# Re-ordering the opening, the scan's first steps and the output projection of a three-block model, with eight idle matmuls at the start

## The chip, the cores and the metric

The kernel runs on one core of one Trainium2 chip. The metric is the device time of one execution in microseconds. A core has five engines with queues of their own: TensorE (PE; its weight loads are shown as PEld), VectorE (DVE), ScalarE (ACT), GpSimd (POOL) and SyncE (SP), which issues the weight transfers. They wait for each other through semaphores that the kernel sets and waits for by hand.

## What is computed

Two token-mixing blocks with their MLPs, and then a third block, over 256 tokens (272 with 16 meta tokens in front) of width 1024, all in float32. What the change touches lies in the first mixer, a state-space one, and in the attention of the second, which works on query blocks of 16, 128 and 128 tokens; h is rms-normed ahead of both:

```python
def ssd_mixer(h, w_in, conv_w, conv_b, dt_bias, a_log, d_skip, norm_g, w_out):
    zxbcdt = h @ w_in
    z, xbc, dt = jnp.split(zxbcdt, [SSD_D_INNER, SSD_D_INNER + SSD_CONV_DIM], axis=-1)
    xbc = jax.nn.silu(causal_depthwise_conv(xbc, conv_w, conv_b))
    dt = jax.nn.softplus(dt.astype(f32) + dt_bias.astype(f32))
    ...
    decay = jnp.exp(jnp.where(causal, a_cs[..., :, None] - a_cs[..., None, :], -jnp.inf))
    cb = jnp.einsum('bclgn,bcsgn->bcgls', c_c, b_c)
    y_diag = jnp.einsum('bcgjls,bcsgjp->bclgjp', cb[:, :, :, None] * decay, xdt)
    ...
    g = (y * jax.nn.silu(z)).reshape(bsz, L, SSD_GROUPS, SSD_D_INNER // SSD_GROUPS)
    g = g * lax.rsqrt(jnp.mean(g * g, axis=-1, keepdims=True) + EPS)
    return (g.reshape(bsz, L, SSD_D_INNER) * norm_g) @ w_out

def mla_mixer(h, ...):
    ...
    p = jax.nn.softmax(jnp.where(mask, sc, -jnp.inf), axis=-1)
    outs.append(jnp.einsum('bhqk,bkhd->bqhd', p, v[:, :e]))
```

## The kernel before

Activations lie with features on the 128 partitions and tokens along the row. Every large product is made three times, in a reduced float32 format: a value is split into a high part (rounded by ACT) and a low part (what is left, a subtraction on DVE or POOL), and `tile` (L446) issues high x high, high x low and low x high (L458 to L460) for each of the 8 steps of the inner dimension. One *page* is 128 output columns of weights: 512 KB, loaded by SP into one of four slots of `w_raw`, split by `hi` (ACT, L942) and `lo` (DVE L1379, POOL L1998), and read by 24 matmuls. There are 344 pages, in one fixed order. The slot's next load waits for `lo`, its next `hi` for the matmuls (`w_used`). `lin_chunk` takes two pages into one half of the PSUM tile `lin`; the other half is drained meanwhile (`drained`, by the chunk's parity).

**The opening.** h arrives in four transfers. ACT rounds each of its 8 tiles (`xr_hi`, in the memory of `g_hi`, L974) and squares it (L955), DVE makes the low parts (`raw_lo`, L1411) and adds the squares up in fours (`add_squares`, L1415). PE makes the dt columns (24 matmuls of 32 rows, L500 to L502), with two matmuls by ones for the norm's sum between them (`first_stat`, L490), and two pages of x, all from the un-normed h. Then `norm_inv` (ACT L965, L967) gives `r_inv`, and DVE and ACT make the normed input `x_hi`, `x_lo` (L1402, L984, L1406) that all later chunks read.

**The scan** has 8 groups in slots 0 to 7, three chunks each (x; B and C; z), and runs one group's later steps beside the next group's projections; `slot` on each engine writes that order out by hand. The steps that matter here are: `conv0` (ACT L1019) and `conv` (DVE L1481) drain a chunk; `clamp` (L1491), `sigmoid` (ACT L1000 to L1004) and `silu` (L1495) follow; `cb_products` and `x_transposes` (PE); `decay_logs` (ACT L1033) reads `acs_bc`, which POOL fetches by a transfer for each group (`acs_rows`, L2006) once the group before has used it; `decay` (L1043), `head_mix` (L1519) and `y_products` (PE L558 to L564), whose third step has 16 tokens only; and a norm per group (`group_stat` L545, `g_low` L1525). A slot begins on PE with a chunk that waits until `conv` of the slot before has drained its half of `lin`.

**The output projection** (`sout`) reads groups 0 to 3 as half 0 and 4 to 7 as half 1, and stops 2 steps short of the end of half 1 until the last group's norm is done. DVE then adds the result to h (`add_pair`, L1601).

**Values of the attention** (`values`, L778 to L782) have a first step over 16 key tokens.

## Time and profile before

| | us |
|---|---|
| median of 3 runs (1121.63 to 1124.04) | 1123.45 |
| the profiled execution | 1122.35 |
| its span, first to last instruction | 1120.7 |
| PE busy in the span | 1095.9 |
| DVE, ACT, POOL busy | 769.1, 655.1, 165.3 |

The profiled execution lies 1.1 us under the median, and 1.65 us of it lie outside the span. PE is busy in nearly all of the span, so time is lost where PE stands still or runs at its lower clock. Of the 40 equal slices of the span (28 us each), only the first (6 tenths), the second (8) and the last (8) show PE below nine tenths. The mean granted clock over the span is 0.997, and the stretches from 30 to 40 us and from 40 to 50 us have 0.83.

A row of the timeline reads: start in us, length in us, engine, line, operation, output<-input, shape, and in brackets how long the engine had stood still before and what ended that. Matmuls are pipelined, so the step from one start to the next, not the length, is what one costs.

### The profile page before, as it was taken

Reading aid. Unit: us, or ns where it says so; the run is one execution under the profiler, and the core shown is the slowest. Engines: PE = TensorE matmul, PEld = TensorE weight load, DVE = VectorE, ACT = ScalarE, POOL = GpSimd, SP = SyncE. Lnnn points to the kernel's source line nnn. Section 1 sums busy time; section 2 is a strip of 40 time slices with the busy share of each in tenths; the row PEclk is TensorE's granted clock in tenths of the full one; section 3 lists DMA queues with packets and bytes.
Section 4 is the critical chain, followed back from the end, with each engine's and each line's share of the span. In section 5 each row is a group of like instructions: output and inputs, shape, how many; then the busy total and the mean of one; then the engine's idle time right before and its main releaser. Section 6 shows DMA issues by size and latency. Waiting matters only on the chain.

```text
span 1120.7 us, 23950 instructions
## 1 busy us (share of the span) xinstructions
PE 1095.9 (98%) x8935; PEld 1064.0 (95%) x8935; DVE 769.1 (69%) x1156; ACT 655.1 (58%) x1077; POOL 165.3 (15%) x150
## 2 busy tenths in 40 slices
PE   6899999999999999999999999999999999999998
PEld 6899999899999999988799999999989999999998
DVE  7789989868665455588686665557787587666543
ACT  7699998655545444477565554446546656555332
POOL 0344444408000000112020000000003201000000
PEclk9899999999999999999999999999999999999999
DMA  6444454484545554433255555555444555555552
GB/s 229 161 164 170 152 189 151 129 252 165 185 170 170 178 178 167 153 132 113 77 188 188 183 183 183 188 182 176 171 135 156 175 185 188 184 180 188 184 185 92
DMA packets 53226, 189.96 MB, mean 170 GB/s; under 512 B 5920, under 2 KB 7200, under 8 KB 53168
## 3 DMA queue, kind: packets, MB, share of 16 engines
...
q8 instruction: 38, 0.62, 0.2%
...
## 4 chain that ended last, share of the span: by engine, by line
PE 73%; DVE 11%; ACT 9%; issue 4%; DMA 1%; POOL 1%; ACTq 1%; DVEq 0%; SPq 0%; POOLq 0%
PE lin L458 22%; PE lin L460 22%; PE lin L459 22%; DVE w_lo L1379 3%; ACT w_hi L942 2%; DVE cv L1481 1%; ACT dd L1033 1%; DVE sg L1491 1%; DMA acs_bc<-acs_dram 1%; ACT cv L1019 1%; PE lin L676 1%; ACT sg L1002 1%; PE lin L677 1%; PE lin L678 1%; ACT ee L1043 1%
## 5 line engine op out<-in xcount | busy, mean ns | idle before, releaser
L1379 DVE TENSOR_TENSOR w_lo<-w_raw,w_hi 128x1024 fp32r<-128x1024 f32 (+3 forms) x318 | 383.9, 1209 | 254.1 <-ACT w_hi L942 254.0
L942 ACT ACTIVATE w_hi<-w_raw 128x1024 fp32r<-128x1024 f32 (+2 forms) x342 | 352.1, 1034 | 224.8 <-PE lin L460 222.1
L458 PE MATMUL lin<-x_hi,w_hi 128*128 128x256 f32 (+1 forms) x1504 | 433.7, 288 | 6.0 <-DVE cv L1481 2.7
L460 PE MATMUL lin<-x_hi,w_lo 128*128 128x256 f32 (+1 forms) x1504 | 429.7, 286 | 0.0
L459 PE MATMUL lin<-x_lo,w_hi 128*128 128x256 f32 (+1 forms) x1504 | 428.8, 285 | 0.0
L458 PEld LDWEIGHTS lin<-x_hi,w_hi 128*128 128x128 f32 x1504 | 285.0, 189 | 8.3 <-POOL w_lo L1998 2.9
L460 PEld LDWEIGHTS lin<-x_hi,w_lo 128*128 128x128 f32 x1504 | 285.2, 190 | 0.0
L459 PEld LDWEIGHTS lin<-x_lo,w_hi 128*128 128x128 f32 x1504 | 284.5, 189 | 0.6
L460 PE MATMUL lin<-hid_hi,w_lo 128*128 128x256 f32 (+1 forms) x768 | 218.2, 284 | 0.0
L459 PE MATMUL lin<-hid_lo,w_hi 128*128 128x256 f32 (+1 forms) x768 | 217.9, 284 | 0.0
L458 PE MATMUL lin<-hid_hi,w_hi 128*128 128x256 f32 (+1 forms) x768 | 217.4, 283 | 0.0
L460 PEld LDWEIGHTS lin<-hid_hi,w_lo 128*128 128x128 f32 x768 | 145.1, 189 | 0.0
L458 PEld LDWEIGHTS lin<-hid_hi,w_hi 128*128 128x128 f32 x768 | 145.0, 189 | 0.0
L459 PEld LDWEIGHTS lin<-hid_lo,w_hi 128*128 128x128 f32 x768 | 144.3, 188 | 0.0
L1990 POOL TENSOR_TENSOR h_sq<-h_sq 128x256 f32<-128x256 f32 (+1 forms) x35 | 30.7, 876 | 451.8 <-ACT h_sq L955 450.4
L1122 ACT ACTIVATE relu<-lin 128x512 f32<-128x512 f32 (+1 forms) x48 | 29.1, 606 | 82.6 <-PE lin L460 82.6
L1998 POOL TENSOR_TENSOR w_lo<-w_raw,w_hi 128x1024 fp32r<-128x1024 f32 x24 | 60.0, 2499 | 86.5 <-ACT w_hi L942 86.3
L951 ACT ACTIVATE x_hi<-h,vecs 128x256 fp32r<-128x256 f32 (+2 forms) x40 | 20.3, 507 | 43.2 <-DVE h L1642 38.3
L458 PE MATMUL lin<-g_hi,w_hi 128*128 128x272 f32 x144 | 42.5, 295 | 2.1 <-DVE g_lo L1525 1.0
L1625 DVE TENSOR_TENSOR hid_lo<-relu_sq,hid_hi 128x512 f32 (+1 forms) x48 | 34.4, 717 | 11.2 <-DVE relu_sq L1621 11.2
L460 PE MATMUL lin<-g_hi,w_lo 128*128 128x272 f32 x144 | 41.7, 289 | 0.0
L459 PE MATMUL lin<-g_lo,w_hi 128*128 128x272 f32 x144 | 41.5, 288 | 0.0
...
## 6 DMA issues: line engine op xcount, KB each, us to landing
w_raw<-w SPq DMA_DIRECT2D x342, 512.0 KB, 3.3
...
```

The costliest lines, as they stand in the source:

```text
L458: mm3(o, wh, xh, start=first and i == 0, stop=False)
L459: mm3(o, wh, xl, start=False, stop=False)
L460: ins = mm3(o, wl, xh, start=False, stop=last and i == kts - 1)
L676: mm3(o, lh, wh, start=i == 0, stop=False)
L677: mm3(o, ll, wh, start=False, stop=False)
L942: a(w_hi[pg.slot][:, 0:n], w_raw[pg.slot][:, 0:n], ACT.Copy).then_inc(w_hi_done, pages)
L951: a(x_hi[:, kt.value, 0:width(norm)], h[:, kt.value, tokens(norm)], ACT.Copy, scale=gain(norm, kt.value)).then_inc(xh_done, 1)
L1122: a(relu[i][:, :, 0:n], linp(k, slice(0, n)), ACT.Relu).then_inc(drained[k.parity], 1)
L1379: tt(w_lo[pg.slot][:, 0:n], w_raw[pg.slot][:, 0:n], w_hi[pg.slot][:, 0:n].bitcast(F32), ALU.subtract)\
L1625: tt(hid_lo[:, bass.ds(at.value, 2), 0:n], relu_sq[i][:, :, 0:n], hid_hi[:, bass.ds(at.value, 2), 0:n].bitcast(F32), ALU.subtract).then_in ...
L1990: tt(h_sq[:, 0, 0:n], h_sq[:, 0, 0:n], h_sq[:, kt, 0:n], ALU.add).then_inc(hsum_done, 1)
L1998: tt(w_lo[pg.slot][:, 0:n], w_raw[pg.slot][:, 0:n], w_hi[pg.slot][:, 0:n].bitcast(F32), ALU.subtract)\
```

## The change

It has four parts.

**Opening.** PE first issues eight matmuls of ones by ones into `ps4`, whose result nobody reads, and then sums the norm itself: eight matmuls, one for each tile of squares, ahead of the dt columns; two of the squares are made by DVE, six by ACT, and the additions on DVE are gone. ACT makes most of the rounded tiles before the squares, and `norm_inv` comes ahead of the split of page 3. The dt steps on DVE move in between the low parts of the normed input. x of group 0 is scaled into two PSUM banks, not into `y2`. DVE, not POOL, makes the low part of page 7 (second page of z of group 0); POOL instead makes that of page 8, and fetches `acs_bc` first.

**First slots.** Slot 0 has an order of its own (`first_slot`): on DVE both convolutions come one after the other, then the clamps; on ACT the pages' splits come first, then the sigmoids. The `decay_logs` of group 0 move from the end of slot 0 into slot 1.

**Output projection.** `group_stat(At(7))` comes one tile earlier, the fourth tile stops after 3 steps of half 1 and makes its other 5 at the end, and DVE's first `add_pair` comes ahead of a page's low part.

**16-row steps.** `x_tok[:, 2, :]` and `p_t0` are zero below their 16 rows, and the last step of `y_products` and the first of `values` read all 128 rows.

```diff
+WARM = 8
-        first_xs = y2
+        first_xs = (ps5, ps6)
-        p_t0 = [sb(f"p_t0{i}", [META, T2], F32, mla) for i in range(2)]
+        p_t0 = [sb(f"p_t0{i}", [P, T2], F32, mla) for i in range(2)]
...
             pe.wait_ge(ones_set, 1)
+            for i in range(WARM):
+                nc.tensor.matmul(ps4[:, 0:P], ones0, ones0, start=True, stop=True)
+            for kt, (squared, count) in enumerate(((hsq_done, 1), (hsq_done, 2), (hsq_dve, 1), (hsq_dve, 2),
+                                                   (hsq_done, 3), (hsq_done, 4), (hsq_done, 5), (hsq_done, 8))):
+                pe.wait_ge(squared, count)
+                ins = nc.tensor.matmul(ps7[:, 0:T], ones0, h_sq[:, kt, :], start=kt == 0, stop=kt == KD - 1)
+            ins.then_inc(stat_done, 1)
             pe.wait_ge(w_lo_done[0], 1)
-                if kt in (2, 3):
-                    first_stat(kt - 2)
...
-                        ins = nc.tensor.matmul(o[rows, 256:T], x_tok[0:META, 2, j * HD:(j + 1) * HD],
-                                               mm[0:META, j, 416:432], start=False, stop=True)
+                        ins = nc.tensor.matmul(o[rows, 256:T], x_tok[:, 2, j * HD:(j + 1) * HD],
+                                               mm[:, j, 416:432], start=False, stop=True)
...
             pe.wait_ge(gl_done, 14)
-            for j in range(3):
-                sout(0, j, 1, 0, 6)
-            group_stat(At(7))
-            sout(0, 3, 1, 0, 6)
+            sout(0, 0, 1, 0, 6)
+            sout(0, 1, 1, 0, 6)
+            group_stat(At(7))
+            sout(0, 2, 1, 0, 6)
+            sout(0, 3, 1, 0, 3)
             pe.wait_ge(gl_done, 16)
-            for j in range(4):
+            for j in range(3):
                 sout(0, j, 1, 6, 2)
+            sout(0, 3, 1, 3, 5)
...
                 if has_lin and early:
-                    if s.base:
-                        hi((c + 2).page(0))
+                    hi((c + 2).page(0))
                     conv0(s, 0)
+                    decay_logs(g, 0)
+                    hi((c + 2).page(1))
+                    decay_logs(g, 1)
...
+            def first_slot():
+                s, c = At(0), At(C_GRP)
+                conv0(s, 0)
+                hi((c + 3).page(0))
+                conv0(s, 1)
+                hi((c + 3).page(1))
+                hi((c + 4).page(0))
+                hi((c + 4).page(1))
+                for pair in range(2):
+                    act.wait_ge(clamped, pair + 1)
+                    sigmoid(sg[:, 2 * pair:2 * pair + 2, :], sg_step, At(3 * pair))
...
+            def first_slot():
+                s = At(0)
+                conv(s, 0)
+                conv(s, 1)
+                for pair in range(2):
+                    both = slice(2 * pair, 2 * pair + 2)
+                    clamp(sg[:, both, :], cv[:, both, :]).then_inc(clamped, 1)
+                z_clamp(s)
+                lo(At(C_GRP + 4).page(0))
+                silu(s, 0, xs_s[0][:, :, :], cv[:, 0:2, :], sg[:, 0:2, :])
+                dt_columns()
...
             for i in range(2, 8):
+                j = i // 4 * 2 + i % 2
+                if i == 2:
+                    add_pair(At(K_SOUT + j), 2 * (C_SOUT + i + 1), j, slice(0, T))
                 lo(At(C_SOUT + 2 + i).page(0))
-                if i % 4 >= 2:
-                    j = i // 4 * 2 + i % 2
+                if i % 4 == 3 or i == 6:
                     add_pair(At(K_SOUT + j), 2 * (C_SOUT + i + 1), j, slice(0, T))
...
-            slot(At(0), has_stat=False)
+            pool.wait_ge(dt_dve, 5)
+            pool.dma_start(acs_dram, acs[:, :]).then_inc(acs_out, 16)
+            pool.wait_ge(acs_out, 16)
+            acs_rows(At(0))
+            lo(At(C_GRP + 3).page(0))
+            lo(At(C_GRP + 3).page(1))
+            lo(At(C_GRP + 4).page(1))
```

PE's first instructions: before, the dt columns (`lin`, three matmuls a tile) with the first of the two sums between them:

```order
L500 MATMUL lin<-g_hi,w_hi0 32x272
L501 MATMUL lin<-g_lo,w_hi0 32x272
L502 MATMUL lin<-g_hi,w_lo0 32x272
L490 MATMUL ps7<-h_sq,mm 128x272
L500 MATMUL lin<-g_hi,w_hi0 32x272
L501 MATMUL lin<-g_lo,w_hi0 32x272
L502 MATMUL lin<-g_hi,w_lo0 32x272
L490 MATMUL ps7<-h_sq,mm 128x272
```

and of the change:

```order
L494 MATMUL ps4<-mm 128x128 x8
L498 MATMUL ps7<-h_sq,mm 128x272 x8
L505 MATMUL lin<-g_hi,w_hi0 32x272
L506 MATMUL lin<-g_lo,w_hi0 32x272
L507 MATMUL lin<-g_hi,w_lo0 32x272
L505 MATMUL lin<-g_hi,w_hi0 32x272
L506 MATMUL lin<-g_lo,w_hi0 32x272
```

The norm's sum (`ps7`) now stands ahead of all dt columns, in eight matmuls instead of two, with the idle eight (`ps4`) ahead of it.

ACT around the border of slots 0 and 1. `dd` is written by `decay_logs`, `cv` by `conv0`, `sg` by the sigmoids, `ee` by `decay`. Before:

```order
L1033 ACTIVATE dd<-acs_bc,cols 16x16
L1033 ACTIVATE dd<-acs_bc,cols 128x272
L1033 ACTIVATE dd<-acs_bc,cols 128x144
L1033 ACTIVATE dd<-acs_bc,cols 16x16
L1033 ACTIVATE dd<-acs_bc,cols 128x272
L1033 ACTIVATE dd<-acs_bc,cols 128x144
L1033 ACTIVATE dd<-acs_bc,cols 16x16
L942 ACTIVATE w_hi3<-w_raw3 128x1024
L942 ACTIVATE w_hi0<-w_raw0 128x1024
L1019 ACTIVATE cv<-lin,vecs 128x272 x2
L1043 ACTIVATE ee<-dd 128x864 x2
```

and of the change:

```order
L1023 ACTIVATE sg<-sg 128x544
L947 ACTIVATE w_hi0<-w_raw0 128x1024
L1038 ACTIVATE cv<-lin,vecs 128x272 x2
L1052 ACTIVATE dd<-acs_bc,cols 128x272
L1052 ACTIVATE dd<-acs_bc,cols 128x144
L1052 ACTIVATE dd<-acs_bc,cols 16x16
L1052 ACTIVATE dd<-acs_bc,cols 128x272
L1052 ACTIVATE dd<-acs_bc,cols 128x144
L1052 ACTIVATE dd<-acs_bc,cols 16x16
L947 ACTIVATE w_hi1<-w_raw1 128x1024
L1052 ACTIVATE dd<-acs_bc,cols 128x272
L1052 ACTIVATE dd<-acs_bc,cols 128x144
```

The twelve `dd` instructions of group 0 stood ahead of slot 1's `conv0`; they now stand behind it, with one page's split (`w_hi1`) between their halves.

DVE in the output projection: `z_s1` and `g_lo` are the last group's norm, `h<-h,lin` is `add_pair`. Before:

```order
L1573 TENSOR_TENSOR z_s1<-y2,g_inv 128x544
L1525 SCALAR_TENSOR_TENSOR g_lo<-z_s1,vecs,g_hi 128x272 x2
L1379 TENSOR_TENSOR w_lo2<-w_raw2,w_hi2 128x1024
L1601 TENSOR_TENSOR h<-h,lin 128x544
L1379 TENSOR_TENSOR w_lo3<-w_raw3,w_hi3 128x1024
L1389 SCALAR_TENSOR_TENSOR x_lo<-h,vecs,x_hi 128x272 x2
```

and of the change:

```order
L1624 TENSOR_TENSOR z_s1<-y2,g_inv 128x544
L1558 SCALAR_TENSOR_TENSOR g_lo<-z_s1,vecs,g_hi 128x272 x2
L1646 TENSOR_TENSOR h<-h,lin 128x544
L1407 TENSOR_TENSOR w_lo2<-w_raw2,w_hi2 128x1024
L1407 TENSOR_TENSOR w_lo3<-w_raw3,w_hi3 128x1024
L1417 SCALAR_TENSOR_TENSOR x_lo<-h,vecs,x_hi 128x272 x2
```

The addition to h moved ahead of the low part of the page that `w_lo2` holds.

## Rows read from the trace of the kernel before

**Rows 1.** The page: busy time of the engines; ACT's group of high parts.

```profile
PE 1095.9 (98%) x8935; PEld 1064.0 (95%) x8935; DVE 769.1 (69%) x1156; ACT 655.1 (58%) x1077; POOL 165.3 (15%) x150
...
L942 ACT ACTIVATE w_hi<-w_raw 128x1024 fp32r<-128x1024 f32 (+2 forms) x342 | 352.1, 1034 | 224.8 <-PE lin L460 222.1
```

**Rows 2.** Timeline of PE, first dt columns: start, length, engine, line, operation.

```profile
9.50 0.40 PE L500 MATMUL lin<-g_hi,w_hi 128*32 128x272 f32 x1 [9.50 <-DVE w_lo L1379]
9.71 0.43 PE L501 MATMUL lin<-g_lo,w_hi 128*32 128x272 f32 x1
...
14.58 0.28 PE L501 MATMUL lin<-g_lo,w_hi 128*32 128x272 f32 x1
14.70 0.29 PE L502 MATMUL lin<-g_hi,w_lo 128*32 128x272 f32 x1
```

**Rows 3.** Timeline of PE, stalls in slots 0 to 2 (brackets: idle before).

```profile
33.39 0.39 PE L458 MATMUL lin<-x_hi,w_hi 128*128 128x272 f32 x1 [2.72 <-POOL w_lo L1998]
...
40.40 0.39 PE L458 MATMUL lin<-x_hi,w_hi 128*128 128x272 f32 x1 [1.79 <-DVE cv L1481]
...
65.08 0.39 PE L458 MATMUL lin<-x_hi,w_hi 128*128 128x272 f32 x1 [0.94 <-DVE cv L1481]
```

**Rows 4.** Timeline of ACT and DVE, opening.

```profile
13.91 0.49 ACT L965 ACTIVATE r_ln<-ps,eps_t 128x272 f32<-128x272 f32 x1 [1.06 <-PE ps L490]
...
11.94 2.36 DVE L1379 TENSOR_TENSOR w_lo<-w_raw,w_hi 128x1024 fp32r<-128x1024 f32 x2
...
14.89 0.44 DVE L1402 TENSOR_TENSOR h_sq<-h,r_inv 128x272 f32<-128x272 f32 x1 [0.59 <-ACT r_inv L967]
...
28.62 2.52 DVE L1481 SCALAR_TENSOR_TENSOR cv<-y,vecs,cv 128x271 f32<-128x271 f32 x6
```

**Rows 5.** Timeline of ACT, POOL and DVE, slot 1.

```profile
43.92 3.78 ACT L1033 ACTIVATE dd<-acs_bc,cols 128x272 f32<-128x272 f32 x12 [0.57 <-DVE cols L1465]
...
51.06 0.57 POOL L2006 DMA_DIRECT2D acs_bc<-acs_dram  x1
...
56.33 1.95 ACT L1033 ACTIVATE dd<-acs_bc,cols 128x272 f32<-128x272 f32 x6 [1.30 <-DMA acs_bc<-acs_dram]
...
62.43 2.51 DVE L1481 SCALAR_TENSOR_TENSOR cv<-lin,vecs,cv 128x271 f32<-128x271 f32 x6
```

**Rows 6.** Timeline of PE, ACT and DVE, slots 4 and 5.

```profile
132.89 0.39 PE L458 MATMUL lin<-x_hi,w_hi 128*128 128x272 f32 x1
...
155.49 0.39 PE L458 MATMUL lin<-x_hi,w_hi 128*128 128x272 f32 x1
...
127.54 1.03 ACT L1019 ACTIVATE cv<-lin,vecs 128x272 f32<-128x272 f32 x2
...
150.22 1.02 ACT L1019 ACTIVATE cv<-lin,vecs 128x272 f32<-128x272 f32 x2
...
136.71 3.05 DVE L1525 SCALAR_TENSOR_TENSOR g_lo<-z_s,vecs,g_hi 128x272 f32 x2
...
151.91 2.51 DVE L1481 SCALAR_TENSOR_TENSOR cv<-lin,vecs,cv 128x271 f32<-128x271 f32 x6
```

**Rows 7.** Timeline of PE, output projection.

```profile
224.73 0.62 PE L545 MATMUL ps<-y_sum,cst 128*128 128x272 f32 x2
...
228.65 0.39 PE L458 MATMUL lin<-g_hi,w_hi 128*128 128x272 f32 x1 [1.04 <-DVE g_lo L1525]
...
232.76 0.39 PE L458 MATMUL lin<-g_hi,w_hi 128*128 128x272 f32 x1 [0.83 <-DVE h L1601]
```

**Rows 8.** Timeline of PE, 16-row steps of the scan and of the attention.

```profile
108.99 0.29 PE L564 MATMUL ps<-mm,x_tok 16*64 16x16 f32 x4
109.21 0.68 PE L558 MATMUL ps<-mm,x_tok 128*64 128x272 f32 x4
...
509.15 0.65 PE L778 MATMUL ps<-p_t,v_tok 16*64 16x256 f32 x4
509.73 0.65 PE L780 MATMUL ps<-p_t,v_tok 128*64 128x256 f32 x4
```

145 lines of the change are left out of this document (75 added, 70 removed).

## The prediction

> **What bounds the kernel now.** I read the page first: PE is busy for 1095.9 of 1120.7 us [rows 1], so only some 25 us of standing still, and what a lower clock costs, can be won at all. Next the waits of PE and its timeline, which say where those 25 us are. The reader is to see in [rows 2] that PE stands for the first 9.50 us, and that its first matmuls then start 0.21 to 0.23 us apart (9.50, 9.71), the later ones 0.12 (14.58, 14.70): granted 1.2 GHz first, 2.4 GHz after, with 272 columns in each. [Rows 3] show three more stalls, 2.72 us (for a low part that POOL makes), 1.79 us and 0.94 us (for DVE's convolution). After the first two, the next 17 matmuls start 0.227 us apart, not 0.126, so each also costs 1.7 us of clock. [Rows 7] show two stalls of 1.04 and 0.83 us in the output projection. Everywhere else up to 300 us PE starts a matmul every 0.126 us. Third, the timelines of ACT, DVE and POOL, for what PE waits for. All sums below stand against the profiled execution, 1122.35 us, whose span is 1120.7; it lies 1.1 us under the median of the three runs.
>
> **The opening, up to slot 1's first chunk.** Before, PE starts that chunk at 40.40. Now step by step.
>
> The last square on ACT moves from the end of its list to 10.3 us, only a little earlier than before. PE sums each square as it comes. One such matmul of 272 float32 columns is two passes of 0.227 us, as the group sum at 224.73 [rows 7] shows (0.47 us until the next one), so the sum is complete at 10.9. ACT is then in a page's high part until 11.2 (1034 ns, [rows 1]); `r_ln` starts there and not at 13.91 [rows 4], and `r_inv` is there at 12.1, 2.7 us sooner. The part of page 3 that is queued behind `norm_inv` on ACT is done at 13.1; PE wants it at 17, so that costs nothing.
>
> The idle matmuls are 8 of 128 columns, 0.43 us each at the low clock: 3.4 us from 1.3 to 4.7, ahead of the first square at 5.0. They delay nothing. What they buy is the clock: dt columns at 0.124 instead of 0.227. From 10.9, 24 matmuls take 3.0 us and the two pages of x 6.05, so PE is through at 20.0 (before 21.26). That lead is not the point, because the next chunks wait for DVE.
>
> DVE starts on `r_inv` at 12.4, after a page's low part (two took 2.36 us [rows 4]), and not at 14.89. From there to the first convolution at 28.62 it needed 13.7 us [rows 4]. The change adds two low parts in that stretch (page 3 and page 7, 1.13 each), takes out a 0.4 us wait, and a gap of 0.6 us after the scan, and adds 0.2 for x in two pieces: 12.4 + 13.7 + 2.3 - 0.8 = 27.6 to 27.9. Writing x to PSUM is not in the trace; between the 0.63 us it took to SBUF and twice that I take 0.8. On the way, PE's third chunk (pages 6, 7) can start when x is drained, at 26.8 (before 27.4), and finds page 7 ready, because DVE made it and not POOL: the 2.72 us and their clock loss go. It ends at 32.9. The two convolutions, 2.6 us each with their gap (2.51 us also where POOL runs beside one that reads PSUM [rows 5]), end at 33.1, and slot 1's first chunk starts at 33.3, not 40.40. It runs at full clock and ends at 39.4, not 48.07: **8.7 us** ahead. What POOL is queued for is not late: page 8's low part is ready at 31.3, page 9's at 33.6 and page 11's at 36.6, wanted at 33.3, 36.3 and 42. POOL's wait for its own transfer (2 us) holds only these.
>
> **Slot 1 gives a part back.** The `dd` instructions moved here, 3.78 us for twelve [rows 5], stand behind slot 1's `conv0`. That matters because group 1's `acs_bc` can only be fetched when group 0's `dd` are done: `conv0` 0.93, six `dd` 1.86, a page 0.96, six `dd` 1.95, from 39.5 to 45.2; the transfer takes 51.06 to 56.33, 5.3 us [rows 5], so it lands at 50.6, **5.7 us** before the old 56.33. From the landing to the end of the convolution that PE waits for it was 62.43 + 2.51 - 56.33 = 8.6 us: dd, sigmoid, silu, a low part, the convolution, one waiting for the other [rows 5]. So slot 2 starts at 59.3, where it was 65.08 [rows 3]. PE, done with slot 1 at some 54.8, stands there for 4.5 us, longer than at any of the four stalls that go. The clock will fall there, for another 1.7 us by [rows 3], so PE itself is only 4.0 us ahead then, ACT, DVE and POOL 5.7.
>
> **Slots 2 to 7.** PE's slot takes 155.49 - 132.89 = 22.60 us [rows 6]. ACT repeats after 150.22 - 127.54 = 22.68 us [rows 6], and it isn't waiting for PE: its waits in slot 5 are for the transfer of `acs_bc` and for a clamp on DVE. The convolution ends at 154.42, PE wants it at 155.49. So the other engines go round by themselves at almost PE's pace, with a slack of 1.1 us. Anything that makes PE faster here by more than its slack meets that loop. With the 1.7 us that PE lags behind, the slack is 2.8, and no stall is due in these slots.
>
> **16-row steps.** In [rows 8] the 16-row step takes from 108.99 to 109.21, 0.22 us for four matmuls of 16 columns, and the step ahead 0.35 where its columns are worth 0.24; PEld stands 0.20 us before each of the 16 such steps. With 128 rows the loads can run ahead as for the other steps. I take 0.35 us a group; the bounds are 0, if the loads take that time anyway, and 0.45. In slots 2 to 7 that is 2.1 us, so PE comes out 4.0 + 2.1 = 6.1 us ahead, and the loop is 5.7 ahead: the loop decides, 5.7 us. In the attention the step of 256 columns takes 509.73 - 509.15 = 0.58 us, and the next, with 128 rows and as many columns, 0.48 [rows 8]: 0.10 us for each of 8 pairs, **0.8 us**; bounds 0 and 1.5. The two zeroings on POOL there and one on DVE at the start have no one waiting for them.
>
> The Trainium skill, TensorEngine Tiling (Array Packing), Key Properties, has it that a change of the tiling mode drains the engine. The 0.58 against 0.48 us agrees with that. By this rule one change of mode goes in the attention, which is what I take, and two per half group in the scan; taken alone it would let PE gain 0.45 us a group, and the sum would not change, because the loop is behind it.
>
> **Output projection.** PE's sum for the last group comes one tile earlier, at 221.9 instead of 224.73 [rows 7], which fills most of a wait for a page. Its chain (until 228.62: ACT, DVE, ACT, DVE) took 3.9 us from the start of the sum; it ends at 225.8. PE has 2.27 + 1.13 us of tiles to put there, to 225.8, so the 1.04 us stall goes. Then three tails of 0.76 us and one of 1.9 end at 230.0; `add_pair` runs after the second, at 228.2, and the low part behind it on DVE is ready at 229.4. What started at 232.76 [rows 7] starts at 230.0: **2.7 us**; bounds 1.2 (the `add_pair` stall only) and 2.8.
>
> **The sum.** 5.7 + 2.7 + 0.8 = 9.2 us. 1122.35 - 9.2 = 1113.2 us. Pages after this are PE's own, and nothing waits there that moved.
>
> **The rivals.** (1) *The loop isn't a bound.* Then PE's own lead counts, 6.1 to 6.7, and with 1.5 in the attention the gain is 11: 1111.3. For it: the two leads are close. Against: its waits in slot 5. Chance 0.13.
>
> (2) *The clock does not hold.* The idle eight end before the squares begin, and the squares, some 0.45 us every 0.75, leave gaps up to 0.9 us before 10.9. Stalls of 1.79 us brought 1.2 GHz [rows 3]. Then the sum of squares, sixteen passes at the low clock, is complete at 12.2, all on DVE is 1.0 to 1.2 later, and slot 2 too: 1114.3. Chance 0.15.
>
> (3) *The wait in slot 1 is longer.* A `dd` or the transfer late, or DVE held by POOL where page 10, 12 or the clamps meet POOL's three parts in a row (29 to 37 us): the lead is 3 rather than 5.7, 1115.9. The same if the projection gives half. Chance 0.15.
>
> (4) *Slower than before: DVE and POOL collide in each slot.* DVE's two `g_lo` take 3.05 us in slot 5 [rows 6], against 0.92 in the output projection, while POOL runs beside them. The two loops are now in another phase only if PE's lag shifts a wait. A second such collision in each of slots 2 to 7 costs 2.1 x 6 = 12.8 us, and the result is 1126. It decides from 9.2 / 6 = 1.5 us a slot. Against: nothing in the loop is re-ordered from slot 2 on. Chance 0.03.
>
> The Trainium skill, GPSIMD Engine Reference, lists the SBUF interfaces as shared with VectorE, contended by instructions with two SBUF inputs or in a two-port mode. The 3.05 us agree. By itself it would change only this rival.
>
> (5) *The change doesn't do what it says*: the gains of the opening are all taken back by slot 1, because the fetch of `acs_bc` is not earlier than before. It would need `dd` to end at 51 us. Then only 2.7 + 0.8 are left, less a longer clock loss: 1121 or so, on the edge of no change. Chance 0.04.
>
> **How the numbers follow.** The forecast has 0.50, the rivals 0.13, 0.15, 0.15, 0.03 and 0.04. The likeliest time is 1113.2 us. The unknown costs alone give 1111 to 1115.5; the range to the neighbours, with the noise of some 1 us that the three runs show, is 1109.8 to 1118. A measurement of this kernel can tell about 0.2%, 2.2 us. Faster by more: 0.93; within: 0.04; slower: 0.03.
>
> **What would show it.** In the changed kernel's profile PE should start the first chunk of slot 1 at 33 to 34 us (opening right), stand 4 to 5 us before slot 2 at 59 to 60 (slot 1 right), with matmuls 0.227 us apart after that; the steps between dt matmuls should be 0.124 (clock right); no stall over 0.3 us in slots 3 to 7; ACT's period 22.7; the stalls of [rows 7] gone; the step at [rows 8] 0.48. The prediction is wrong if page 7 or x is late at 27 us, if the transfer of `acs_bc` for group 1 is issued after 47 us, or if PE stalls again in a later slot.

## The result, and the profile after

| | before, us | changed, us |
|---|---|---|
| median (runs) | 1123.20 (4) | 1112.51 (4) |
| lowest to highest | 1121.63 to 1124.04 | 1112.07 to 1112.80 |
| the profiled execution | 1122.35 | 1112.07 |
| its span | 1120.7 | 1110.4 |

The ratio is 0.9906, 95% interval 0.9893 to 0.9920: the change makes the kernel 10.6 us faster (9.0 to 12.0). The forecast was 1113.2 us in a range of 1109.8 to 1118. One execution of the changed kernel's second series (e9_same below) took 2729 us, for a reason that the records don't show, and is left out everywhere. PE's busy time hardly moved (answers [rows 1]); what fell is the time in which PE stands, from 1120.7 - 1095.9 = 24.8 to 1110.4 - 1096.7 = 13.7 us:

```profile
PE 1096.7 (99%) x8963; PEld 1068.2 (96%) x8963; DVE 766.3 (69%) x1154; ACT 654.2 (59%) x1075; POOL 165.1 (15%) x152
```

Both kernels issue the same matmuls in nearly the same order, so the start of the k-th matmul of a kind can be compared between the two traces. This is the most useful view here: the *lead*, its start in the trace of before minus its start in the trace after, at the first matmul of a stretch.

| first matmul of | before, us | lead, us |
|---|---|---|
| the chunk ahead of slot 1 | 33.39 | 4.02 |
| slot 1 | 40.40 | 7.49 |
| slot 2 | 65.08 | 7.23 |
| slot 2, second chunk | 72.81 | 5.72 |
| slot 3, 4, 5 | 87.7, 110.3, 132.89 | 6.12, 6.51, 6.92 |
| slot 6, 7 | 155.49, 178.1 | 7.32, 7.72 |
| the output projection | 200.7 | 7.98 |
| its chunk at 224 (and 232.76) | 224.0 (232.76) | 7.19 (9.92) |
| the first MLP | 257.1 | 9.63 |
| the attention's first scores | 483.5 | 9.64 |
| the MLP after the attention, and the end | 599.2 | 10.31, 10.28 |

The opening, in the timeline of PE of the changed kernel (start, length, engine, line, operation, in brackets the idle time before and who ended it; answers [rows 2] and the first two of [rows 3]):

```profile
1.30 3.67 PE L494 MATMUL ps<-mm 128*128 128x128 f32 x16 [1.30 <-DVE mm L1424]
4.95 2.49 PE L498 MATMUL ps<-h_sq,mm 128*128 128x272 f32 x8
7.64 1.18 PE L498 MATMUL ps<-h_sq,mm 128*128 128x272 f32 x4 [0.21 <-ACT h_sq L960]
9.42 1.18 PE L498 MATMUL ps<-h_sq,mm 128*128 128x272 f32 x4 [0.59 <-ACT h_sq L960]
...
10.56 0.29 PE L506 MATMUL lin<-g_lo,w_hi 128*32 128x272 f32 x1
10.69 0.28 PE L507 MATMUL lin<-g_hi,w_lo 128*32 128x272 f32 x1
...
32.91 0.39 PE L462 MATMUL lin<-x_hi,w_hi 128*128 128x272 f32 x1
```

The dt matmuls step by 0.13 us from the first on, which is 2.4 GHz, and slot 1 starts at 32.91 without a stall. Next, the only stall over 0.6 us that is left between the start and 600 us, before slot 2, and PE's clock behind it (answers the third line of [rows 3]):

```profile
57.85 0.39 PE L462 MATMUL lin<-x_hi,w_hi 128*128 128x272 f32 x1 [2.48 <-DVE cv L1514]
58.08 0.28 PE L463 MATMUL lin<-x_lo,w_hi 128*128 128x272 f32 x1
...
59.34 0.42 PE L464 MATMUL lin<-x_hi,w_lo 128*128 128x272 f32 x1
59.55 0.43 PE L462 MATMUL lin<-x_hi,w_hi 128*128 128x272 f32 x1
...
62.27 0.43 PE L462 MATMUL lin<-x_hi,w_hi 128*128 128x272 f32 x1
62.50 0.41 PE L463 MATMUL lin<-x_lo,w_hi 128*128 128x272 f32 x1
```

The first twelve matmuls after the stall still step by 0.126 us (2.4 GHz), then some fifteen by 0.227 (1.2 GHz): 15 x 0.10 = 1.5 us, the fall of the lead from 7.23 to 5.72.

The same stretch on POOL and ACT, answers [rows 5]: ACT first stands 2.31 us for a weight page, with slot 0's six sigmoids behind it in its list; POOL issues group 1's fetch at 45.20, ACT's `dd` waits for it until 49.20, 0.73 us.

```profile
33.36 1.06 ACT L947 ACTIVATE w_hi<-w_raw 128x1024 fp32r<-128x1024 f32 x1 [2.31 <-DMA w_raw<-w]
...
45.20 0.59 POOL L2050 DMA_DIRECT2D acs_bc<-acs_dram  x1 [7.45 <-ACT dd L1052]
...
47.80 0.66 ACT L1023 ACTIVATE z_sg<-z_sg 128x544 f32<-128x544 f32 x1
49.20 1.94 ACT L1052 ACTIVATE dd<-acs_bc,cols 128x272 f32<-128x272 f32 x6 [0.73 <-DMA acs_bc<-acs_dram]
```

That page's transfer was issued at 27.49 us and landed at 33.33, after 5.85 us, while POOL's fetch of group 0's `acs_bc`, 544 KB issued at 26.95, was under way until 33.14; the transfers issued at 19.58 and 22.23 took 3.08 and 3.31. From this landing on, ACT works through its list with no wait but the 0.73 us, up to the convolution step that slot 2 needs.

Slots 5 and 6 on PE and ACT, answers [rows 6]:

```profile
125.97 0.39 PE L462 MATMUL lin<-x_hi,w_hi 128*128 128x272 f32 x1
...
148.17 0.39 PE L462 MATMUL lin<-x_hi,w_hi 128*128 128x272 f32 x1
...
120.39 1.03 ACT L1038 ACTIVATE cv<-lin,vecs 128x272 f32<-128x272 f32 x2
...
143.07 1.03 ACT L1038 ACTIVATE cv<-lin,vecs 128x272 f32<-128x272 f32 x2
```

PE's slot now takes 22.20 us where it took 22.60. ACT still goes round in 22.68, and leads ACT of before by 127.54 - 120.39 = 7.15 and 150.22 - 143.07 = 7.15 us. PE's lead grows by 0.40 in each slot. The most that it can reach is ACT's lead and the slack that PE had in the kernel before; where PE does stand for the loop, in e9_same below, that is 7.05 for PE with 6.10 for ACT, about 0.9 us more. So PE meets the loop at 8.0 to 8.1, which is the beginning of the projection (7.98). Then the projection and the attention, answering [rows 7, 8]: two short stalls at the entrance of the projection, none where the two long ones were, and the first step over all 128 rows.

```profile
204.07 0.73 PE L548 MATMUL ps<-y_sum,cst 128*128 128x272 f32 x2 [0.33 <-POOL y_sum L2064]
...
210.03 0.39 PE L462 MATMUL lin<-g_hi,w_hi 128*128 128x272 f32 x1 [0.27 <-DVE g_lo L1558]
...
499.37 0.65 PE L783 MATMUL ps<-p_t,v_tok 128*64 128x256 f32 x4
499.85 0.60 PE L785 MATMUL ps<-p_t,v_tok 128*64 128x256 f32 x4
...
528.06 0.65 PE L783 MATMUL ps<-p_t,v_tok 128*64 128x256 f32 x4 [0.48 <-DVE p_t L1835]
```

### The profile page after: what moved, and what is told of

The parts are those of the page before. It is cut to its first block, busy times and chain, and to the rows that moved or that the text cites. A ratio compares the mean times of both kernels' runs of the same rounds, so it can differ in the third digit from the quotient of the medians.

```text
span 1110.4 us, 24004 instructions
## 1 busy us (share of the span) xinstructions
PE 1096.7 (99%) x8963; PEld 1068.2 (96%) x8963; DVE 766.3 (69%) x1154; ACT 654.2 (59%) x1075; POOL 165.1 (15%) x152
## 4 chain that ended last, share of the span: by engine, by line
PE 79%; DVE 11%; ACT 5%; issue 3%; DMA 2%; POOL 0%; ACTq 0%; DVEq 0%; SPq 0%
PE lin L462 25%; PE lin L464 25%; PE lin L463 25%; DVE w_lo L1407 3%; DMA w_raw<-w 1%; ACT w_hi L947 1%; DVE s_m L1817 1%; ACT dd L1052 1%; DVE p_t L1835 1%; DVE x_lo L1417 1%; DVE cv L1514 0%; ACT pr L1328 0%; PE ps L561 0%; DMA acs_bc<-acs_dram 0%; DVE q_ss L1760 0%
## 5 line engine op out<-in xcount | busy, mean ns | idle before, releaser
L1672 DVE TENSOR_TENSOR hid_lo<-relu_sq,hid_hi 128x512 f32 (+1 forms) x48 | 34.4, 717 | 11.2 <-DVE relu_sq L1668 11.2
```

The lines of the kernel that those rows point to most:

```text
L1672: tt(hid_lo[:, bass.ds(at.value, 2), 0:n], relu_sq[i][:, :, 0:n], hid_hi[:, bass.ds(at.value, 2), 0:n].bitcast(F32), ALU.subtract).then_in ...
```

## The experiments

Twelve kernels. "Lead" below is against the profiled execution of the changed kernel unless it says otherwise, negative where the experiment is later.

| kernel | median, us (runs) | lowest to highest | ratio to before (95%) |
|---|---|---|---|
| changed | 1112.51 (4) | 1112.07 to 1112.80 | 0.9906 (0.9893 to 0.9920) |
| e1_warm0 | 1113.78 (4) | 1113.24 to 1114.03 | 0.9924 (0.9908 to 0.9941) |
| e2_scan16 | 1113.98 (4) | 1113.65 to 1115.60 | 0.9931 (0.9915 to 0.9948) |
| e3_values16 | 1113.53 (4) | 1112.43 to 1113.57 | 0.9919 (0.9903 to 0.9936) |
| e4_proj | 1115.18 (4) | 1115.03 to 1116.23 | 0.9940 (0.9923 to 0.9956) |
| e5_acs2 | 1112.72 (4) | 1111.73 to 1113.45 | 0.9910 (0.9894 to 0.9927) |
| e6_idle | 1113.70 (4) | 1113.41 to 1113.80 | 0.9922 (0.9905 to 0.9938) |
| e7_before16 | 1122.34 (10) | 1121.38 to 1124.02 | 0.9998 (0.9989 to 1.0008) |
| e8_fetch | 1112.63 (4) | 1111.98 to 1112.96 | 0.9913 (0.9897 to 0.9930) |
| e9_same | 1113.42 (4) | 1112.67 to 1113.87 | 0.9919 (0.9904 to 0.9934) |
| e10_warm0b | 1112.81 (5) | 1112.20 to 1113.03 | 0.9910 (0.9897 to 0.9924) |
| e11_hi | 1112.08 (4) | 1109.94 to 1113.61 | 0.9910 (0.9895 to 0.9925) |
| e12_swap | 1111.54 (4) | 1110.57 to 1112.15 | 0.9901 (0.9884 to 0.9917) |

e9_same is the changed kernel itself once more. Its four executions and the first four together give 1112.07 to 1113.87 us, and its ratio is 0.9919 where the first was 0.9906. The kernels were measured in five series (changed; e1 to e4; e5 to e8; e9 to e11; e12), in which the kernel before had medians of 1122.16 to 1123.20, and "above the changed kernel" below compares medians of two series. So a difference of 1 us between two kernels of this table is at the edge of what the times alone can tell. The leads in the traces say more, and which stretch.

### The eight idle matmuls: e1_warm0, e10_warm0b

```
-WARM = 8
+WARM = 0
```

> The changed kernel without the eight idle matmuls of ones. If they buy the clock (the prediction's reading), the squares' sums and the first dt matmuls start 0.22 to 0.23 us apart and not 0.12, the sum of squares is complete 0.3 to 1.2 us later, the first chunk of slot 1 starts at 33.2 to 34.1 us and not at 32.91, and the kernel is 0.3 to 1.2 us slower. Rival: the squares alone bring the clock up before the dt columns, or DVE's chain hides it; then slot 1 starts within 0.1 us of 32.91 and the time is the same within 0.3 us.

Measured: 1113.78 us. That looked like 1.3 us, but the trace speaks against the reading. PE's first matmuls, the squares' sums and the first dt column:

```profile
5.48 5.63 PE L498 MATMUL ps<-h_sq,mm 128*128 128x272 f32 x16 [5.48 <-ACT h_sq L960]
10.75 0.49 PE L505 MATMUL lin<-g_hi,w_hi 128*32 128x272 f32 x1
```

The dt matmuls that follow step by 0.12 to 0.13 us here too: the clock comes up within the sixteen passes of the squares, whose own step falls from 0.45 to 0.23 us at 8.79 us. What is lost is that the passes themselves run slower, until 10.75 instead of 10.24, and slot 1 starts at 33.41, 0.50 later. But slot 2 starts 1.87 later, and the other 1.4 us come from elsewhere: the weight page for which ACT stands ahead of slot 0's sigmoids was there 1.84 us later than in the changed kernel's first trace (its transfer took 7.18 us).

```profile
35.20 1.06 ACT L947 ACTIVATE w_hi<-w_raw 128x1024 fp32r<-128x1024 f32 x1 [3.63 <-DMA w_raw<-w]
```

The kernel was run again beside the changed one.

> The kernel of e1_warm0 again (no idle matmuls at the start), beside the changed kernel on one chip. If the eight idle matmuls are worth anything it is 0.5 to 1.5 us slower than e9_same, as e1_warm0's 1113.78 beside 1112.51 us has it; if that difference was the scatter of the opening, it is the same within 0.4 us.

Measured: 1112.81 us, and the changed kernel on the same chip (e9_same) 1113.42. Slot 1 starts at 33.65 us here, and at 33.05 in e9_same, but slot 2 at 58.50 and 58.92. So without the idle matmuls slot 1 starts at 33.41 and 33.65, with them at 32.91 to 33.44 (ten traces of the changed order), and what follows, ACT's list behind that page (taken up at 34.28 and 34.34 us), does not keep the difference. Over both pairs no effect on the time can be told. The first expectation's claim, 0.3 to 1.2 us slower, is not supported; "the same within 0.3 us" is not shown either.

### The changed kernel again: e9_same

> The changed kernel itself again, to have it and e10_warm0b and e11_hi on one chip and to see how far the opening and slot 1 differ from one execution to the next. Both theories: 1112 to 1113 us. In the traces so far slot 1 starts between 32.91 and 33.44 us although nothing ahead of it was edited in most of them; this one shows whether 32.91 is the rule. If the ten idle matmuls of e6_idle themselves made that kernel slower, this one starts slot 1 before 33.2.

Slot 1 started at 33.05 us, so the 33.44 of e6_idle is on the late side of a scatter that comes with the arrival of h: its first transfer lands at 3.94 us in the changed kernel's first trace and at 4.07 to 4.39 in the others with idle matmuls, and the last square's sum starts at 9.42 there and at 9.54 to 9.95 in these. Slot 2 started at 58.92, 1.07 later than in the first trace, after a stall of 3.00 us, and the clock did **not** fall behind it.

Most of that 1.07 is the page again, taken up at 34.34 us and not at 33.36. All twelve traces of the changed order agree on it. ACT takes this page up at 33.36 to 35.20 us. In the nine with one `acs_bc` tile slot 2 starts 24.05 to 24.59 us later, which is ACT's wait for group 1's fetch (0.41 to 0.96) and 23.62 to 23.76 us of its list; in e5_acs2, e8_fetch and e11_hi, where the fetch comes in time, it starts 23.52 to 23.54 us later. So the start of slot 2, and with it the lead of the loop, hangs on when this page lands. No experiment moved its transfer or the fetch beside it, so that the fetch delays it is argued from the times alone. Slot 0's first clamp ends at 33.36, so an earlier page would have let the sigmoids begin up to about 0.9 us earlier in the first trace, and 2.3 in e1_warm0: an estimate, from 34.32 and 36.17, where they began, and 33.36 and 33.87, where the clamp ended.

The lead of e9_same was +0.45 in slot 3 and then went down again, through stalls that the first trace did not have:

```profile
148.44 0.39 PE L462 MATMUL lin<-x_hi,w_hi 128*128 128x272 f32 x1 [0.38 <-DVE cv L1514]
...
171.11 0.39 PE L462 MATMUL lin<-x_hi,w_hi 128*128 128x272 f32 x1 [0.40 <-DVE cv L1514]
...
193.74 0.36 PE L462 MATMUL lin<-g_hi,w_hi 128*128 128x272 f32 x1 [0.36 <-issue]
```

This is the loop as a bound. Where the clock holds, PE catches up with it and stands; where it falls, PE arrives 1.5 us later and does not stand. The time is the same: the changed kernel's four timed executions have a mean clock of 0.998 (1112.07, 1112.73) and 1.000 (1112.80, 1112.29).

### One part undone at a time: e2_scan16, e3_values16, e4_proj

```
-  nc.tensor.matmul(o[rows, 256:T], x_tok[:, 2, ...], mm[:, j, 416:432], ...)
+  nc.tensor.matmul(o[rows, 256:T], x_tok[0:META, 2, ...], mm[0:META, j, 416:432], ...)
```

> The changed kernel with the scan's third step over 16 rows again (nothing else undone). If ACT's loop decides, as the prediction had it, PE loses its 0.35 to 0.40 us a group inside its slack and the kernel is 0 to 0.8 us slower. If PE's own lead counts, as the trace of the changed kernel suggests (its lead over the kernel before grows by 0.40 us in each of slots 2 to 7), it is 2.0 us or more slower: six slots of 0.40, and up to 0.8 for the groups 0 and 7 outside them, less what slot 2's stall hides: 2.0 to 3.0 us.

Measured: 1113.98 us, 1.5 above the changed kernel. The lead falls by 0.40 in each slot to -2.67 at the start of the projection, then comes back to -1.83 at 216.8 us and -1.58 behind the projection, because the two short stalls at its entrance are gone. 0.41 of these 1.58 us were there before slot 2, so the steps cost about 1.2. Neither expectation was right: PE's pace counts here, but not all of it. In this execution the clock fell, so PE was behind the loop and its pace mattered; the next experiment is the other case.

```
 # the kernel before, with x_tok[:, 2, :] zeroed below 16 rows, and
-  nc.tensor.matmul(o[rows, 256:T], x_tok[0:META, 2, ...], mm[0:META, j, 416:432], ...)
+  nc.tensor.matmul(o[rows, 256:T], x_tok[:, 2, ...], mm[:, j, 416:432], ...)
```

> The kernel before with one edit, the scan's third step over all 128 rows. TensorE gains 0.40 us a group, 2.8 us over groups 0 to 6. If the loop decides, only the slack of 1.1 us is open: 0.6 to 1.3 us faster, with stalls at the beginning of slots 5 to 7. If TensorE's own pace counts: 2.4 to 2.8 us faster, no such stalls.

Measured: 1122.34 against 1122.69 us, ratio 0.9998. Against its own base PE gains 0.40 in slots 2, 3 and part of the next, in all 1.0 us, then stands, and gives the rest back in the projection (lead over before 1.53 in slot 5, 1.42 in slot 7, 0.58 behind the projection, of which 0.50 were there from the opening):

```profile
154.02 0.39 PE L458 MATMUL lin<-x_hi,w_hi 128*128 128x272 f32 x1 [0.40 <-DVE cv L1482]
...
176.68 0.39 PE L458 MATMUL lin<-x_hi,w_hi 128*128 128x272 f32 x1 [0.37 <-DVE cv L1482]
...
199.31 0.36 PE L458 MATMUL lin<-g_hi,w_hi 128*128 128x272 f32 x1 [0.36 <-issue]
```

Of 2.8 us that TensorE saves, nothing arrives: the loop decides. The expected 0.6 to 1.3 was still too much, because it left out what the projection takes back.

```
-  nc.tensor.matmul(o, vt[:, e, :], p_t0[e][:, :], start=True, stop=False)
+  nc.tensor.matmul(o, vt[0:META, e, :], p_t0[e][0:META, :], start=True, stop=False)
```

> The changed kernel with the first step of the attention's values over 16 rows again. Prediction's term: 0.8 us slower (0.10 for each of 8 pairs); the trace of the changed kernel gives a lead that grows by 0.67 us between the products before the attention and the next MLP. Rival: a wait elsewhere takes it over, and the time is the same within 0.2 us.

Measured: 1113.53 us, 1.0 above the changed kernel. The lead is -0.68 from slot 2 on (a later opening and a stall of 2.86 there), -0.86 before the attention and -1.46 behind it: 0.6 us belong to the attention.

```
-            sout(0, 0, 1, 0, 6)
-            sout(0, 1, 1, 0, 6)
+            for j in range(3):
+                sout(0, j, 1, 0, 6)
             group_stat(At(7))
-            sout(0, 2, 1, 0, 6)
-            sout(0, 3, 1, 0, 3)
+            sout(0, 3, 1, 0, 6)
             pe.wait_ge(gl_done, 16)
-            for j in range(3):
+            for j in range(4):
                 sout(0, j, 1, 6, 2)
-            sout(0, 3, 1, 3, 5)
...
-                if i == 2:
-                    add_pair(...)
                 lo(At(C_SOUT + 2 + i).page(0))
-                if i % 4 == 3 or i == 6:
+                if i % 4 >= 2:
                     add_pair(...)
```

> The changed kernel with the output projection's order of the kernel before, on TensorE and VectorE. The prediction's term is 2.7 us slower, bounds 1.2 and 2.8. The trace of the changed kernel has a lead of 8.0 us before the projection and 9.64 after it, which would make it 1.6 us. If it is 2.7 the order was worth what was predicted, and something else in that stretch took 1.1 us back; if 1.6, one of the two old stalls was already gone by the new phase of the engines or the new order has a stall of its own.

Measured: 1115.18 us, 2.7 above the changed kernel. Both stalls of [rows 7] are back:

```profile
222.22 0.39 PE L462 MATMUL lin<-g_hi,w_hi 128*128 128x272 f32 x1 [1.04 <-DVE g_lo L1556]
226.34 0.39 PE L462 MATMUL lin<-g_hi,w_hi 128*128 128x272 f32 x1 [0.84 <-DVE h L1644]
```

The lead goes from -0.76 at 216.8 us to -3.50 and comes back to -3.22: 2.5 us for this part. So it is worth what was predicted, and the 1.65 us that the lead over before gains from 7.98 to 9.63 is 2.73 less 0.79 at the entrance (7.98 to 7.19, close to the loop's 7.15) and 0.29 near the end. What takes the last 0.3 is probably a page that comes late. ACT, changed kernel, waits for the transfers of weights that share the DMA engines with POOL's four transfers of `bias_mask`:

```profile
225.42 1.06 ACT L947 ACTIVATE w_hi<-w_raw 128x1024 fp32r<-128x1024 f32 x1 [2.24 <-DMA w_raw<-w]
229.84 1.06 ACT L947 ACTIVATE w_hi<-w_raw 128x1024 fp32r<-128x1024 f32 x1 [3.35 <-DMA w_raw<-w]
```

In e5_acs2 the second wait was 4.40 us, and TensorE stood for 1.20 us behind it. The four transfers of `bias_mask` are under way from 213.71 to 231.92 us, and the two pages for which ACT waits took 10.10 and 13.39 us, where those issued at 206.87 and 208.00 took 3.17 and 4.44. That these transfers are the cause was not tested by moving them.

### What the loop is made of: e5_acs2, e8_fetch, e6_idle, e11_hi, e12_swap

```
-        acs_bc = sb("acs_bc", [P, HPG, T], F32, ssd)
+        acs_bc = [sb(f"acs_bc{i}", [P, HPG, T], F32, ssd) for i in range(2)]   # by g.parity
...
-                if g.base:
-                    pool.wait_ge(dd_done, g.times(2).value)
+                if g.base >= 2:
+                    pool.wait_ge(dd_done, g.times(2, -2).value)
```

> The changed kernel with two acs_bc tiles by the group's parity, so that group 1's fetch no longer waits for group 0's dd instructions (in the trace of the changed kernel it is issued at 45.20 us and lands at 49.2). Theory A (the fetch sets slot 1's tail, and after it ACT's loop decides): issue at 37.8, dd of group 1 at 46.7 instead of 49.20, TensorE's stall before slot 2 is 0 to 0.6 us and not 2.48, its clock stays up, so TensorE starts slot 2 some 2.3 us earlier and is 3.8 us ahead of the changed kernel in slot 3; the loop is only 2.3 ahead, so stalls come in slots 4 to 7 that take 1 us or more of it back, and the kernel is 2.2 to 2.8 us faster. Rival B (the loop is no bound): all 3.8 us stay. Rival C: another wait (the sigmoid, conv0 behind a page) is as late, and the gain is under 0.5 us.

Measured: 1112.72 us, no gain. Group 1's fetch was issued at 38.1 and was there in time, yet `dd` of group 1 started at 49.5 and PE's slot 2 at 58.14. The expectation had put ACT's arrival at that point 2.8 us too early, mainly by leaving out z's sigmoid (2 us); besides, the page came at 34.61, 1.25 later than in the first trace. Rival C is what happened.

```
 # as e5_acs2, and in POOL's slot
                     lo((c + 3).page(1))
+                    acs_rows(s + 1)       # was at the start of slot s + 1
                     lo((c + 4).page(1))
```

> As e5_acs2, and from slot 1 on each fetch is issued one low part earlier on GpSimd, so that ACT need not wait for it (0.7 to 0.9 us in each slot of the changed kernel). If this wait is a part of ACT's period of 22.68 us, the period falls to 22.2 us or less, TensorE meets no stall in slots 3 to 7, and all of its 3.8 us stay: 3.5 to 4 us faster than the changed kernel. Rival: ACT's period is set by what else it waits for (the clamp on VectorE takes up what the fetch gives), it stays at 22.6 to 22.7, and the gain is that of e5_acs2, 2.2 to 2.8 us.

Measured: 1112.63 us. ACT in slot 1:

```profile
48.48 0.66 ACT L1023 ACTIVATE z_sg<-z_sg 128x544 f32<-128x544 f32 x1
49.05 1.93 ACT L1052 ACTIVATE dd<-acs_bc,cols 128x272 f32<-128x272 f32 x6
```

No wait is left there, and slot 2 starts at 57.70, 0.15 earlier than in the changed kernel, although its page came 0.80 later (34.16): counted from the page, the fetch was worth 0.95 us. From the page on ACT is simply never free until it has done the convolution's first step that slot 2 needs. In the later slots the wait for the fetch is gone too, and the same time has come back as a wait for DVE's clamp. The waits from 60 to 200 us (engine, line, for whom: us, times, longest), first of the changed kernel, then of e8_fetch:

```profile
ACT sg L1019 <- DVE sg L1524: 4.9, 6, 1.1
ACT dd L1052 <- DMA acs_bc<-acs_dram: 4.7, 6, 1.3
```

```profile
ACT sg L1019 <- DVE sg L1524: 10.2, 6, 1.7
```

4.9 + 4.7 = 9.6 against 10.2: ACT's round still takes 22.7 us (its convolutions' first steps start at 111.2, 133.9 and 156.6). The fetch was not on the loop of slots 2 to 7.

```
             slot(At(1), has_stat=False)
+            for i in range(10):
+                nc.tensor.matmul(ps4[:, 0:P], ident, ident, start=True, stop=True)
```

> The changed kernel with ten idle matmuls of 128 columns on TensorE between slot 1 and slot 2, about 2.3 us of the 2.48 us in which it stands still. If they hold the clock, the matmuls after 57.85 us start 0.126 us apart and not 0.227, and TensorE is 1.5 us further ahead in slot 3. Theory A (the loop decides): stalls in slots 4 to 7 take this back, and the time is the same within 0.3 us. Rival B (no bound): 1.5 us faster. Rival C: they don't hold the clock; then it is the same or up to 0.3 slower.

Measured: 1113.70 us. The stall shrank to 0.58 and the clock held, but it also held without idle matmuls in e4, e5, e8, e9, e10 and e11, so the experiment does not show that they held it. What it shows again is theory A: the lead over the start of slot 2 went up by 1.5 us (-1.84 to -0.32) and was taken back by stalls of 0.20 to 0.41 at the start of slots 5 to 7 and of the projection (-1.84 at its beginning). That it is 0.3 to 1.2 us slower than the changed kernel fits its slot 1: it began 0.53 late, and the page was taken up at 35.10, 1.74 late.

```
 # as e8_fetch, and in ACT's slot, from slot 2 on
                     decay(g, 1)
+                    hi((c + 2).page(0))
                     ...                    # z's sigmoid
-                    hi((c + 2).page(0))
                     conv0(s, 0)
```

> The kernel of e8_fetch with one more edit: on ACT, from slot 2 on, the high part of the third chunk's first page stands ahead of z's sigmoid and not behind it, about 2 us earlier. In the trace of e8_fetch VectorE stands 1.67 us in each slot for that high part, and then ACT stands 1.7 us for VectorE's clamp; so the low part comes earlier, the convolution 0.9 us earlier, and ACT's wait shrinks to some 0.8. Theory A (ACT and VectorE waiting for each other make the 22.68 us): ACT's period falls to 22.2 us or less, no stall of TensorE in slots 4 to 7, and the kernel is 1.4 to 2.5 us faster than e8_fetch, 1110 to 1111.2 us. Rival B: the period stays at 22.6 to 22.7 because another work of the round is the limit; same time as e8_fetch. Rival C: the loop is faster, and the transfers of the output projection take the gain back; TensorE stalls for a low part around 230 us, gain under 1 us.

Measured: 1112.08 us, in four executions of 1109.94, 1110.93, 1113.22 and 1113.61. The two fast ones have a mean granted clock of 1.000 and the other two 0.998, so the clock fell in these. In the changed kernel that made no difference; here, with the loop out of PE's way, it can. But it costs 1.5 us and the pairs lie 2.3 to 3.7 apart, and there is no trace of a late one, so the rest is open. In the profiled one (1109.94, span 1108.3) no stall of TensorE is left in slots 3 to 7, and the lead is +1.58 there and +2.12 behind the projection. But ACT's round is 22.7 us as before (109.6, 132.3, 155.0): the edit moved the round once, by 1.7 us between slots 2 and 3 (two squares of ACT are 20.97 apart there), and did not shorten it. Theory A is wrong as it was put. The slot shows why. DVE hardly waits any more (2.1 us in all between 60 and 200 us), and its clamp takes not 0.44, as it does alone, but 2.19 us (DVE and POOL, slot 5):

```profile
136.17 2.19 DVE L1525 TENSOR_SCALAR sg<-cv 128x544 f32<-128x544 f32 x1
...
135.68 2.38 POOL L2043 TENSOR_TENSOR w_lo<-w_raw,w_hi 128x1024 fp32r<-128x1024 f32 x1
```

POOL's low part ends at 138.06, the clamp at 138.36. Wherever a clamp begins in this stretch while POOL makes a low part, it ends just behind POOL. And POOL's low part stands behind `y_sum`, which waits for ACT's square. So the round closes through POOL. In e9_same (ACT, POOL, DVE):

```profile
137.03 0.65 ACT L1086 ACTIVATE h_sq<-y 128x544 f32<-128x544 f32 x1
...
141.21 0.66 ACT L1019 ACTIVATE sg<-sg 128x544 f32<-128x544 f32 x1 [1.06 <-DVE sg L1524]
...
137.76 0.76 POOL L2064 TENSOR_TENSOR y_sum<-h_sq 128x272 f32<-128x272 f32 x1 [2.53 <-ACT h_sq L1086]
138.49 2.38 POOL L2042 TENSOR_TENSOR w_lo<-w_raw,w_hi 128x1024 fp32r<-128x1024 f32 x1
...
139.55 1.62 DVE L1524 TENSOR_SCALAR sg<-cv 128x544 f32<-128x544 f32 x1
```

Square 137.03, `y_sum` 137.76, low part 138.49 to 140.87, clamp until 141.17, sigmoid 141.21, and the next square at 159.69 after 18.48 us of ACT's own list: 22.66 us. One edit takes the low part off this chain:

```
                     # POOL, slots 2 to 7
+                    lo((c + 2).page(1))
                     pool.wait_ge(ysq_done, (gs + 1).value)
                     tt(y_sum[:, :], h_sq[:, 0, :], h_sq[:, 1, :], ALU.add).then_inc(ysum_done, 1)
-                    lo((c + 2).page(1))
```

> The changed kernel with one edit: on GpSimd, in slots 2 to 7, the low part of the third chunk's second page stands ahead of y_sum and not behind it. In the trace of e9_same the round of 22.67 us can be followed as one chain: ACT's square 137.03, GpSimd's y_sum 137.76, GpSimd's low part 138.49 to 140.87, VectorE's clamp of 544 columns, 0.48 us when alone, drawn out from 139.55 to 141.1 beside it, ACT's sigmoid at 141.21, and 16.8 us of ACT's own work until its next square. Theory A (this chain is the round; the fetch and the high part that e8_fetch and e11_hi moved lie on none of its links): the low part runs 0.7 to 1.4 us earlier, the clamp ends 0.8 to 1.2 us earlier, ACT's period falls from 22.67 to TensorE's 22.2, TensorE's stalls at the start of slots 5 to 7 (0.36 to 0.40 each) and at the entrance of the output projection (0.33 and 0.27) go, and the kernel is 1.0 to 1.8 us faster than e9_same, 1111.5 to 1112.3. Rival B: ACT's period stays at 22.6 to 22.7 and the waits come back elsewhere; same within 0.4 us. Rival C: the sum over y_sum on TensorE, wanted at 139.64 us, comes up to 0.7 us late in each slot, and it is slower.

(The 16.8 us in that text are a slip; the trace has 18.48.) Measured: 1111.54 us, 1.9 less than e9_same and 1.0 less than the changed kernel's first median. DVE, ACT and POOL in slot 5, ACT in slot 6:

```profile
136.99 0.81 DVE L1524 TENSOR_SCALAR sg<-cv 128x544 f32<-128x544 f32 x1
...
137.83 0.66 ACT L1019 ACTIVATE sg<-sg 128x544 f32<-128x544 f32 x1 [0.18 <-DVE sg L1524]
...
133.02 1.05 ACT L1038 ACTIVATE cv<-lin,vecs 128x272 f32<-128x272 f32 x2 [0.32 <-PE lin L464]
...
155.30 1.05 ACT L1038 ACTIVATE cv<-lin,vecs 128x272 f32<-128x272 f32 x2 [0.74 <-PE lin L464]
...
135.09 2.40 POOL L2042 TENSOR_TENSOR w_lo<-w_raw,w_hi 128x1024 fp32r<-128x1024 f32 x1 [2.36 <-ACT w_hi L947]
137.46 0.97 POOL L2066 TENSOR_TENSOR y_sum<-h_sq 128x272 f32<-128x272 f32 x1
```

The clamp takes 0.81 us. Between 60 and 200 us ACT waits 1.0 us for clamps (4.9 in the changed kernel) and 2.8 for the fetch (4.7), and 1.7 for PE, which it does not in the changed kernel. Its steps are 155.30 - 133.02 = 22.28 us apart, and its squares 22.10 to 22.28, which is PE's pace of 22.20. The stalls of PE at the entrance of the projection are gone: the lead is -0.56 in slots 3 to 7, as late as its slot 1 made it, +0.83 at 216.0 us and +1.07 behind the projection. That PE does not stand at the start of slots 5 to 7 proves nothing here, since the clock fell before slot 3 as in the changed kernel's first trace; but with the clock fallen, that trace, e1_warm0 and e3_values16 all kept the round of 22.7 us and the two stalls at the entrance (0.33 and 0.27). This is theory A, and the fastest median of all. Its interval overlaps that of the changed kernel (0.9901 against 0.9906 and 0.9919); by the times alone the gain of about 1 us is not certain, the trace shows where it is made. e12's edit together with those of e11 was not run.

## Why the prediction was right, step by step

**The opening: right.** Slot 1 at 33.3 was forecast, and at 32.91 to 33.05 measured. The sum of squares is there a little earlier (`r_ln` starts at 10.64, 11.2 forecast), page 7's and x's stalls and their clock loss are gone. *What the idle matmuls do* was right in size for the clock (0.124 us steps) but not in its cause: without them the dt matmuls have the same steps (e1_warm0). Rival 2, the clock does not hold, did not come. This is the largest term of all, and apart from the idle matmuls its parts were not undone one by one: that the lead arises here is measured (4.02 us at the chunk ahead of slot 1, 7.49 at slot 1), which of the edits made how much of it is read from the timeline alone.

**Slot 1 gives a part back: right in form, 1.5 us wrong in size.** Forecast: slot 2 at 59.3, a stall of 4.5 us, a lead of 5.7. Measured: 57.85, 2.48, and 7.2. The failed term is "the transfer takes 51.06 to 56.33, 5.3 us, so it lands at 50.6": issued at 45.20 as forecast, it was there at 49.20. From that landing to the end of the convolution the 8.6 us taken over from before was right (57.70 - 49.20 = 8.5). But the term was not even the one that decides: ACT came to this point at 48.47, and with the transfer out of the way (e8_fetch) slot 2 came at 57.70. ACT's own list bounds slot 1; of the transfer only 0.7 to 1.0 us were ever in the way. And that list begins with a wait that the prediction put at nothing: the page behind which the sigmoids stand comes at 33.36 us, 2.31 us after ACT was ready for it, and up to 1.84 us later still in other traces of the changed order, with slot 2 as much later.

**Clock behind that stall: right in size, by chance in its coming, and of no weight.** 1.7 us forecast, 1.5 measured, in five of the twelve traces of the changed order; in the other seven it did not fall. The time is the same, since PE meets the loop in slots 5 to 7 instead. With that the prediction's own sign against itself, "if PE stalls again in a later slot", is met in e9_same, the changed kernel itself (0.38 and 0.40 us): the changed kernel kept to "no stall over 0.3 us in slots 3 to 7" only in the trace in which the clock fell.

**Slots 2 to 7: "the loop decides": right.** 22.68 us on ACT and 22.60 on PE were read correctly as two rounds of nearly the same length, and e7_before16 shows the bound at its cleanest: 2.8 us of TensorE's time for nothing. Two things were missing. The lead of the loop was 7.15 us and not 5.7, the same 1.5 as above (in the first trace; the page's landing moves it). And the loop was said to wait "for the transfer of `acs_bc` and for a clamp on DVE"; the transfer could be taken away without a change (e8_fetch), the clamp was one because POOL's low part stood beside it, and this is the collision that rival 4 had feared as a second one. It was already in the round, in each slot, before and after.

The clamp reads one SBUF input and was drawn out from 0.44 to 1.62 and 2.19 us beside POOL; the convolution, which reads PSUM, took 2.51 beside POOL and without it. The Trainium skill, GPSIMD Engine Reference, section 1 (Specifications), has the SBUF interfaces shared with VectorE, with contention for its instructions with two SBUF inputs or in a two-port mode. The rows agree if the clamp runs in a two-port mode, which no row shows directly; the clamp of z, as long but out of PSUM, takes 0.71 us, and the one out of SBUF 0.44.

**16-row steps.** 0.35 us a group forecast, 0.40 measured, with the same bounds; in the attention 0.8 forecast, 0.6 measured (e3_values16; 0.67 in the lead over before), since the first step did fall to 0.48 us but two waits for `p_t` and `k_fin` grew from 0.35 and 0.33 to 0.48 each.

**Output projection: 2.7 us forecast, 2.5 to 2.7 measured** (lead in e4_proj, and its median). Not in the sum: 0.3 us lost again at its end.

**The sum.** 7.2 (loop) + 2.7 - 0.3 (projection) + 0.7 (attention) = 10.3 against 5.7 + 2.7 + 0.8 = 9.2 forecast; measured 10.3 in the span. In the first trace PE's own lead (7.98 at the projection) had just reached the loop's, so that this trace alone would have let rival 1, no loop at all, stand; e7_before16, e6_idle and e9_same rule it out.
